# Six RMS statistics computed in four column tiles of 128 tokens and spread through DRAM

## The reference

```python
def rms_norm(x, g):
    y = x * rsqrt(mean(x * x, axis=-1) + 1e-6)
    return y * g
...
u = rms_norm(h, g_mix)                      # and conv, pooling and gates on u
merged = gates_a * y_conv + gates_b * y_pool
h = h + merged @ w_o
v = rms_norm(h, g_ffn)                      # FFN norm
f = silu(v @ w_ffn_gate) * (v @ w_ffn_up)   # 2816 wide
h = h + f @ w_ffn_down
h = rms_norm(h, g_final)                    # output norm
```

## Time and profile before

| | us |
|---|---|
| median of 3 runs | 989.99 |
| lowest, highest | 989.78, 990.99 |
| the profiled execution's time | 991.0 |
| its span on the slowest core (core 0) | 989.5 |
| spans of the other cores | 985.5 to 989.2 |

### The profile page before, as it was taken

One profiled execution on the slowest core, in us unless ns is written; L12 is line 12 of the kernel. 1 busy time (PEld: TensorE's weight loads), 2 busy tenths in 40 slices (PEclk: granted clock), 3 DMA queues, 4 the chain that ended last, 5 costly groups with the idle time before them and its releaser, 6 DMA issues.

```text
span 989.5 us, 14699 instructions; the slowest of 8 cores (985.5 to 989.5 us)
## 1 busy us (share of the span) xinstructions
PE 962.3 (97%) x5176; PEld 474.0 (48%) x5176; DVE 433.1 (44%) x632; ACT 291.7 (29%) x486; POOL 154.9 (16%) x216
## 2 busy tenths in 40 slices
PE   3999999999899999999999999999999999999996
PEld 2755555554344444444444444444444444444485
DVE  4776689653885323233476212211112211342454
ACT  3853143356952121110544111111111111121121
POOL 3002221124740000001771110110000000000000
PEclk9999999999999999999999999999999999999999
DMA  9705988775773111226965444553222005122222
GB/s 212 233 4 98 217 215 177 231 171 119 132 170 62 22 20 24 32 32 155 356 165 133 74 82 90 101 98 47 34 31 43 12 1 181 75 85 85 85 86 85
DMA packets 41158, 105.81 MB, mean 107 GB/s; under 512 B 5760, under 2 KB 14208, under 8 KB 38400
## 3 DMA queue, kind: packets, MB, share of 16 engines
q0 software_dynamic: 21472, 51.06, 28.7%
q1 hardware_dynamic: 19616, 53.82, 16.3%
HBM read 115.80 MB, written 21.04 MB: 138 GB/s over the span
## 4 chain that ended last, share of the span: by engine, by line
PE 95%; DMA 2%; DVE 1%; POOL 1%; issue 1%; ACT 0%; DVEq 0%; ACTq 0%; POOLq 0%
PE ps L370 92%; PE ps L664 3%; DMA xb<-xp 1%; DMA wslot<-w_pool_out 1%; DVE uT L397 0%; POOL d L384 0%; DVE h2b L397 0%; POOL wslot L199 0%; ACT sqx L381 0%; DVE sqx L384 0%; ACT ps L381 0%; ACT sq L381 0%; DVE h2b L384 0%; DVEq L1033 0%; DVEq L193 0%
## 5 line engine op out<-in xcount | busy, mean ns | idle before, releaser
L370 PE MATMUL ps<-vT,wslot 128*128 128x512 bf16 x1408 | 304.4, 379 | 0.0
L370 PE MATMUL ps<-uT,wslot 128*128 128x416 bf16 (+3 forms) x1536 | 292.3, 349 | 3.1 <-DVE uT L397 2.3
L370 PEld LDWEIGHTS ps<-uT,wslot 128*128 128x128 bf16 x1536 | 151.1, 99 | 140.8 <-issue 12.6
L370 PEld LDWEIGHTS ps<-vT,wslot 128*128 128x128 bf16 x1408 | 137.7, 98 | 167.1 <-issue 1.6
L384 DVE TENSOR_TENSOR fT<-ps,sgf 128x512 bf16<-128x512 f32 x88 | 60.7, 691 | 228.8 <-PE ps L370 228.8
L370 PE MATMUL ps<-fT,wfd 128*128 128x512 bf16 (+1 forms) x880 | 153.2, 336 | 0.0
L381 ACT ACTIVATE sgf<-ps 128x512 f32<-128x512 f32 x88 | 52.5, 597 | 241.5 <-PE ps L370 234.2
L370 PEld LDWEIGHTS ps<-fT,wfd 128*128 128x128 bf16 x880 | 86.1, 98 | 67.8 <-issue 1.7
L370 PE MATMUL ps<-cell,wslot 128*128 128x512 bf16 x512 | 114.8, 379 | 0.0
L397 DVE SCALAR_TENSOR_TENSOR zt<-zt,ps 128x512 f32<-128x512 f32 x64 | 43.9, 687 | 106.1 <-PE ps L370 106.0
L381 ACT ACTIVATE zt<-ps,hb 128x512 f32<-128x512 f32 x64 | 43.9, 691 | 138.1 <-PE ps L370 138.1
(11 more groups left out here) (76 smaller groups left out, 610.6 us busy)
## 6 DMA issues: line engine op xcount, KB each, us to landing
rep<-ad SPq DMA_DIRECT2D x128, 129.5 KB, 4.7
wslot<-w_in POOLq DMA_DIRECT2D x40, 256.0 KB, 7.0
h1d<-h1b SPq DMA_DIRECT2D x4, 2048.0 KB, 10.1
h2b<-h1d SPq DMA_DIRECT2D x4, 2048.0 KB, 13.7
h1b<-xr SPq DMA_DIRECT2D x3, 2048.0 KB, 19.6
out<-h2b SPq DMA_DIRECT2D x3, 2048.0 KB, 8.1
wslot<-w_ffn_gate POOLq DMA_DIRECT2D x22, 256.0 KB, 5.3
wslot<-w_ffn_up POOLq DMA_DIRECT2D x22, 256.0 KB, 5.2
```

Source lines behind the costliest of these rows:

```text
L370: S.op(PE, lambda e: e.matmul(out, lhsT=lhsT, rhs=rhs, start=start, stop=stop), [lhsT, rhs], [out], signal=stop if signal is None else signal)
```

## The change

Six of the statistics, those of blocks 0 and 1 of the FFN norm and of parts 0 to 3 of the output norm, are computed in another way. `rms_spread` makes four products, each of `ones[:, 0:32]` with a quarter of the tokens (128, or 64 where a part has 256 tokens), on four column tiles, so that the sums of quarter j stand in partitions 32j to 32j + 31. ACT's Ln and Exp then run over 128 columns instead of 512. One partition of each quarter is written to a row of a DRAM tensor rd, and the row is read back into all 128 partitions of rb, both on SP's queue, the second waiting for the first. `rms_take`, later in the program, copies rb to PSUM bank 7.

In the w_o stage `rms_spread(b - 1)` stands after tile c = 3 of blocks 1 and 2 and `rms_take` after tile c = 7, where `rms_stat` was. In the down stage `rms_spread` stands where `rms_stat` was, and `rms_take` and `out_norm` move to after tile c = 3 (c = 4 in the last part). The FFN norm's blocks 2 and 3 and the last part of the output keep `rms_stat`.

```diff
+    r_d = nc.dram_tensor("rd", [2 * NB, TT], F32, kind="Internal")
...
+    rq = [at(f"rq{i}", [128, 128], F32, oZ + 38912 + i * 512) for i in range(2)]
+    rb = at("rb", [128, TT], F32, oZ + 38912 + 1024)
...
+    r_sem = [dsem("d_r0"), dsem("d_r1")]
...
+    def rms_spread(n, w_=TT):
+        m = w_ // 4
+        for j in range(4):
+            o, lt, r_ = psum[6][32 * j:32 * j + 32, 0:m], ones[:, 0:32], ac1[n % 2][:, j * m:(j + 1) * m]
+            S.op(PE, lambda e, o=o, lt=lt, r_=r_, j=j: e.matmul(
+                o, lhsT=lt, rhs=r_, start=True, stop=True, tile_position=(0, 32 * j)), [lt, r_], [o])
+        act(rq[0][:, 0:m], psum[6][:, 0:m], AF.Ln, bias=e_rms)
+        act(rq[1][:, 0:m], rq[0][:, 0:m], AF.Exp, scale=-0.5)
+        n_ = rms_spread.n
+        rms_spread.n += 1
+        S.dma(SP, r_sem[0], r_d.ap()[n_:n_ + 1, 0:w_].rearrange("o (j m) -> (o j) m", j=4), rq[1][0::32, 0:m], xw=[("rd", n_)])
+        S.dma(SP, r_sem[1], rb[:, 0:w_], bass.AP(r_d, n_ * TT, [[0, 128], [1, w_]]), xr=[("rd", n_)])
+    rms_spread.n = 0
+
+    def rms_take(w_=TT):
+        act(psum[7][:, 0:w_], rb[:, 0:w_], AF.Copy)
...
             if b > 1:
                 v_norm(b - 2, c)
+            if c == 3 and b in (1, 2):
+                rms_spread(b - 1)
             if c == KC - 1 and b > 0:
-                rms_stat(b - 1)
+                if b < 3:
+                    rms_take()
+                else:
+                    rms_stat(b - 1)
...
             if c == 1 and n > 0:
+                rms_spread(n - 1, parts[n - 1][2])
+            if c == (4 if n == 4 else 3) and n > 0:
                 pb, po, pw_ = parts[n - 1]
-                rms_stat(n - 1, pw_)
+                rms_take(pw_)
                 out_norm(pb, po, pw_)
                 if n == 1:
                     h2_load(3)
```

## The result

| | us |
|---|---|
| changed kernel, median of 6 runs | 1002.2 |
| kernel before, median of 6 runs | 991.1 |
| ratio, 95% interval | 1.0113 (1.0099 to 1.0127) |
| forecast (range) | 990.2 (988.6 to 992.8) |

The account below looks back on a forecast made before the run. TensorE, unbroken from 456 to 980 us, was taken as the bound. Terms: -0.5 (statistics) + 0.2 (rms_spread(0)) + 0.3 (tail) = 0.0, so 990.0 us, written 990.2 for small waits; range 988.6 to 992.8.

Parts of the forecast that it names:

- SP: block 0's h1d store now stands behind the trip of block 1 ... nothing.: FFN norm, SP's queue: store goes out about 502 us; both land by 512 and 522, before the buffer's next writer; no cost.
- a late weight load as a sign of error: Near 520 us: a store that keeps a weight load from landing would show the forecast wrong; no size given.
- the five-step order of high and low passes, 0.74 us: 512-column statistic on TensorE: passes on one tile follow each other, five steps 0.54 us plus 0.20 for tiling changes, against 0.86.
- 5 x 0.12 - 0.10 = 0.5 us: TensorE gain in all: five 512-column statistics gain 0.12 us each, the 256-column one loses 0.10.
- rival B: Edited statistics: all four tiles run at once, passes reordered freely; 2.4 us gained, 0.5 lost, 988.1 us; chance 0.07.
- The two terms beside it: Edited statistics on TensorE: going into column tiles costs 0.10 us and coming out 0.10, 0.20 per visit.
- rival D: Output parts 3 and 4: trip through DRAM late, TensorE and tail wait; 993.2 us with 4 us a transfer; chance 0.10.
- TensorE only when six PSUM banks (10 us) are full: FFN norm's takes: late data hold ACT and v_norm, but TensorE only once six banks fill; priced at nothing.
- the wait at rms_spread(0): Block 0's statistic, moved four tiles forward: TensorE waits for POOL's additions about 0.4 us on core 4; 0.2 us taken.
- no wait at rms_spread(3): Output part 3's spread: its last addition ends about 963.9, needed at 965.2; 1.3 us to spare, no cost.
- ACT's work: Edited statistics: Ln and Exp over 128 columns about 0.36 and 0.29 us plus a copy about 0.60; equal within 0.1.
- the tail's sign: Last part: out_norm after c = 4 runs so near the end that the tail loses 0.3 us.

Follow-up runs that it names:

- the late stores: Kernel before, no statistic changed, h1d stores of blocks 0 and 1 held until block 2's tile c = 4: 1.0079; held until c = 6: 1.0115.
- the FFN half: Changed kernel with only the FFN norm's two statistics spread, the output norm keeping its old ones: 1002.7 us, ratio 1.0123.
- the output half: Changed kernel with only the output norm's four statistics spread, the FFN norm keeping its old ones: 989.4 us, ratio 0.9991.
- one late store: Kernel before, no statistic changed, only block 1's h1d store held until after block 2's tile c = 4: ratio 1.0004.

## Why the prediction was wrong

**The step that failed: "SP: block 0's h1d store now stands behind the trip of block 1 ... nothing."** The place and the time were right (about 502 us forecast, 500.03 measured), and so was the answer to the question that it asked: nothing that reads or writes h1b waits. It asked who needs the buffer, and not who needs the DMA engines. The price of a store was not the error. The median rose from 10.1 us to 20.8 with three out at a time, but the two stores that were priced landed at 513.4 and 521.7 us, where 512 and 522 were forecast. The weights of the next stage, asked for from 506 us on, were not in the sum at all, though the last paragraph named a late weight load as a sign of error. In place of nothing this stage lost 9.0 us by waits for weights and 5.0 by the clock. That late stores do this is shown by the late stores (1.0079 and 1.0115 with no other change), by the FFN half (1.0123) and by the output half (0.9991).

**Why the weights lose so much** may be read from the packets of the 35 us shown above. SP's queue moved 7.68 MB in 533 packets, 14.4 KB each; POOL's weights 1.37 MB in 741, 1.85 KB each. The weights thus had more than half of the packets and 1.37 of 9.05 MB, while the DMA engines were busy without a break from 517 to 532 us. The Trainium skill ("DMA: Bandwidth & Descriptors", Queues, rings and completion order) says that each DMA engine takes turns between its queues packet by packet. The rows agree in kind. That the size of the packets is the reason was not tried by itself, and no run here shows that what the profile counts as a packet is what that page means by one.

**Second step: the five-step order of high and low passes, 0.74 us.** It was 0.36: the term was 5 x 0.12 - 0.10 = 0.5 us and is 2.7, rival B's mechanism. The first (high) passes of all four tiles start within 0.02 us of each other and the second (low) ones after them, so the order in the queue did not chain them. The two terms beside it held: 0.09 us into column tiles (495.18 + 0.215 to 495.48), and 0.11 out of them (495.62 + 0.107 to 495.84).

**The late trip, rival D**, was looked for in parts 3 and 4, where it did not come: there the read takes 3 us and a whole trip 4.7 (Exp's end at 957.96, landing by 962.70), as forecast. It was there in the FFN stage, where the prediction priced it at nothing: 6.4 us for the read of block 1 in the changed kernel, 8.2 for the whole trip (497.79 to 506.0), and a wait of TensorE in two versions in which the stores were in their old place. "TensorE only when six PSUM banks (10 us) are full" did not cover this: a hold of 7.19 us ended in a wait of TensorE, because the backlog lasted through block 3 and delayed block 2's statistic.

**Right:** the wait at rms_spread(0) (0.4 on core 4 forecast, 0.60 measured); no wait at rms_spread(3) on the slowest core; ACT's work (Ln 0.35 and Exp 0.31 over 128 columns); the tail's sign, its size being 0.17 instead of 0.3.

What stays open: what makes the last third of the changed kernel's loss, some 4 us beyond that of the late stores, and how much of the loss would remain if the weights were asked for earlier. Neither was tried.

## What to carry to other kernels

A transfer that waits, put into a queue in program order, delays everything behind it; ask of each transfer behind it not only who needs its data, but also what it will now run beside, and whether that has weights in it that the matrix engine waits for. Price the transfers that the matrix engine waits for by their landing time in the company that they will have, not by a median of quiet ones. And where a change has several places, time each place alone: here four of six cost nothing and two were the whole loss.

## What was unexpected about the hardware

- Eight f32 passes of 128 columns on four column tiles, two on each tile and issued tile by tile, took 0.36 us with the change of tiling in and out; one whole-array f32 statistic of 512 columns takes 0.86. With 64 columns it was 0.25 against 0.43.
- The f32 weight load of 32 columns shows 106 to 110 ns; the bf16 one of the same width shows 97 and the f32 one of 128 columns 190.
- After 4.09 us without a matmul the granted clock of the next 9 us was 0.66; the matmuls of the stage took 5.0 us more in all.
- The eight weight loads of 256 KB issued between 505 and 540 us took 5.9 to 11.6 us each where the 2 MB stores went out one at a time, 8.8 to 13.9 where two of them went out 4.3 us apart (one late store), and 17.2 to 26.2 where three went out within 4 us.
